# New rests for the background steps of a fused two-block kernel, and four tiles at once at the second layer's input product

## The chip, the cores and the metric

The kernel runs on one core of one Trainium2 chip. The metric is the device time of one execution in microseconds (us), the median of several runs.

## The reference

A model of two blocks on 256 positions of width 2048, in float32.

```python
# first block, two layers
mod = silu(c) @ w_ada[l] + b_ada[l]                    # shift, scale, gate
h = rms_norm(x, norm_g[l]) * (1 + scale) + shift
u, z_s, q, k, v, z_a = split(h @ w_in[l])              # 2048 x 6144
y_s = s5_mixer(u, ...) * silu(z_s)                     # state space, gelu, w_glu
y_a = diff_attention(rope(q), rope(k), v, ...) * silu(z_a)   # 8 heads
x = x + gate * (concat([y_s, y_a]) @ w_out[l])
# second block, one layer
z = rms_norm_2(x) @ w_in_2
y_rw, y_mla = rwkv7_mixer(z_rw, ...), mla_mixer(z_mla, ...)
mix = (g_rw * (y_rw @ w_branch_rw) + g_mla * (y_mla @ w_branch_mla)) @ w_out_2
h = x + rms_norm_2(mix); f = (gelu(gate) * val) @ w_down # a 3-tap convolution on w_up's product
h = h + rms_norm_2(f);   h = h + rms_norm_2(sigmoid(h @ w_ple_gate) * (p @ w_ple))
```

## The kernel before

All values are held transposed, width on the 128 partitions and the 256 positions along the row. A weight matrix is read as blocks of 128 by 128, in halves of 8 blocks (512 KB). ScalarE rounds a half to the high part of a split (beat `hi`, 1024 columns), VectorE takes the low part (`lo`), and TensorE does three matmuls of 256 columns for a block: high times high, high times low, low times high. So one block is 3 matmuls, and a tile of 128 output rows is 16 blocks where the inner width is 2048, 8 where it is 1024. The matmuls of all tiles in a row are a **stream**. TensorE's instructions have line 981 (transposes 984), ScalarE's 978, VectorE's 941 to 971, transfers 937, since helpers record them.

The order of the work is written by a planner that runs on the host, `Timeline`. It emits one list of beats, and every engine's program goes through this one list and plays its own part of each beat, in that order, waiting on semaphores. `stream` emits the blocks, and after every `per` blocks it calls `bg()`, which advances each background generator by one `yield`. `per` is 2 for the last 40 tiles of w_in, for w_outa and for the last 40 tiles of w_in2; it is 4 for the first 8 tiles of w_in, for w_glu and for w_outm. The generators are: `s5` (16 batches of the state-space scan; in each, `s5_follow` and the next batch's `s5_prepare` advance together, and every second one has `s5_phases`), `s5_back`, `attention` (8 heads of 15 steps, each head only when its four tiles are out), `modulation` (the product with w_ada for the rest of layer 0 and for layer 1, one 1 MB unit for each unit of the stream), and `rwkv` (8 head pairs of 15 steps, then 7 sequential steps `rw_seq`, then `rw_post` in 24 calls). A **rest** is the number of yields behind a step, so the number of calls until the generator's next beat. `drain` goes on calling `bg` without a stream until a generator is done.

What the steps do, for those that the change touches: in `s5_follow` step 0 TensorE multiplies by the input matrix, 1 ScalarE copies, 2 TensorE transposes, 3 VectorE rotates and scans, 4 TensorE makes y (16 small matmuls, it needs the scan and the taps `WI`, which went through DRAM, `scr_k`), 5 ScalarE copies y, 6 TensorE transposes it, 7 ScalarE copies. In `s5_prepare` 1 to 3 are VectorE's, 4 TensorE transposes, 5 ScalarE copies, 6 TensorE makes the taps, 7 ScalarE copies and POOL stores, 8 POOL loads. In `attention` 0 is the scores, 1, 2, 4 and 6 VectorE's part of the softmax, 3 and 5 ScalarE's, 7 the transposes of the weights, 8 ScalarE's copy, 9 the product with v, 10 ScalarE's squares, 11 POOL's power, 12 ScalarE's scaled copy, 13 its transposes, 14 VectorE's product. In `rwkv` step 0 is TensorE's, 1 and 2 are mostly VectorE's (decay, keys), 3 a product on TensorE and VectorE's factors behind it, 4 to 9 the inverse by doubling, 10 to 12 its application, 13 four products and VectorE's masks, 14 the last products. `s5_phase` is ten instructions of VectorE, `s5_sine` three sines on ScalarE.

The ring in SBUF has four places for halves and one of 1 MB for modulation units (places 4 and 5). SyncE's queue issues all weight loads in the order of use and waits for a place to be free before it goes on to the next.

At the boundary between the layers the last tile of w_outm is added to x, squared and summed, TensorE sums over the partitions (`rms`), ScalarE takes the root, and sixteen tiles of h are made, each by VectorE, ScalarE and VectorE. `warm` loads the table of the root ahead. A name in `PAIRS` with its first unit has the first 32 blocks in the order tile 0 k 0 to 7, tile 1 k 0 to 7, tile 0 k 8 to 15, tile 1 k 8 to 15; one in `QUADS` has the first 64 blocks as k 0 to 3 of four tiles, then k 4 to 7 of the four, and so on, and its weights are packed so (`pack_quads`).

Of the kernel before, what the change touches and what calls it, by code (L numbers as in the profile page):

```python
# [282 lines left out]

PAIRS = (("w_in", 48), ("w_in2", 0), ("w_up", 0))

QUADS = (("w_pg", 0),)


class Tile:
# [8 lines left out]
class Timeline:  # L300
# [240 lines left out]
    def s5(self, l):  # L541
        for i, parts in enumerate((1, 2, 1, 4, 3, 2, 1, 5)):
            for part in range(parts):
                self.add("s5_setup", l, i, part)
                if l or part == parts - 1:
                    yield
                if l:
                    yield
        self.add("s5_first", l)
        for x in self.s5_prepare(l, 0):  # L550
            yield
        for x in self.s5_phases(l, 0):
            yield
        while ("u8", l, 0) not in self.marks:
            yield
        for _ in range(6):
            yield
        for b in range(16):
            both = [self.s5_follow(l, b)] + ([self.s5_prepare(l, b + 1)] if b < 15 else [])
            if b % 2 and b < 15:  # L560
                both.append(self.s5_phases(l, b // 2 + 1))
            while both:
                for g in list(both):
                    if next(g, self) is self:
                        both.remove(g)
                yield
            self.marks.add(("s5", l, b))
# [23 lines left out]
                    yield  # L591

    def s5_phases(self, l, p):
        for _ in range(10 if p else 0):
            yield
        self.add("s5_phase", l, p)
        for _ in range(4):
            yield
        self.add("s5_sine", l, p)
        yield  # L600
# [9 lines left out]
            self.marks.add(("u8", l, half))  # L610

    def s5_prepare(self, l, b):
        for i, rest in enumerate((1, 2, 2, 5, 3, 4, 1, 2, 0)):
            self.add("s5_prep", l, b, i)
            for _ in range(rest):
                yield

    def s5_follow(self, l, b):
        for i, rest in enumerate((2, 3, 1, 5, 2, 3, 1, 2)):
            self.add("s5_run", l, b, i)  # L620
            for _ in range(rest):
                yield

    def attention(self, l):
        for h in range(8):
            while ("w_in", l, 8 + 4 * h + 3) not in self.marks:
                yield
            for i, rest in enumerate((2, 2, 2, 2, 2, 2, 4, 2, 2, 2, 1, 2, 2, 2, 1)):
                self.add("att", l, h, i)
                if i == 14:  # L630
                    self.add("part", ("att", l), h)
# [23 lines left out]
    def rwkv(self):  # L655
# [3 lines left out]
        for i in range(8):  # L659
            while i == 3 and ("w_in2", 0, 35) not in self.marks:  # L660
                yield
            for s, rest in enumerate((1, 2, 3, 5, 3, 3, 2, 2, 2, 2, 2, 2, 2, 2, 1)):
                slot = self.take("rw") if s in (1, 3) else None
                self.add("rw", i, s, slot)
                if slot:
# [64 lines left out]
    def run(self):  # L730
# [35 lines left out]
        for l in range(2):  # L766
# [12 lines left out]
                gy = self.s5_back(0)  # L779
                self.bgs += [g5, gy, gm]  # L780
            self.bgs.append(self.load_u8(l))
            self.mod_rest = 2
            self.stream("w_in", l, 48 * l, 0, 8, 16, per=4)
            ga = self.attention(l)
            self.bgs.append(ga)
            self.mod_rest = 5
            self.stream("w_in", l, 48 * l + 8, 8, 40, 16, per=2)
            while l == 0 and ("mod", 0, 11) not in self.marks:
                self.bg()
# [4 lines left out]
            if l == 0:  # L794
                g5, gy = self.s5(1), self.s5_back(1)
                self.bgs += [g5, gy]
            self.mod_rest = 2
            self.stream("w_glu", l, 8 * l, 0, 16, 8, per=4)
            if l:
                self.add("pos2")  # L800
# [1933 lines left out]
def arrange(i):  # L2734
    g = {k: np.asarray(v) for k, v in i.items()}
    A = {}
# [5 lines left out]
    for n, name in enumerate(("lam_q1", "lam_k1", "lam_q2", "lam_k2")):  # L2742
# [11 lines left out]
    A["w_ada"] = np.concatenate([pack_ada(w) for w in g["w_ada"]])  # L2754
    n = np.arange(8)
    order = np.concatenate([n, np.stack([16 + n, 24 + n, 32 + n, 40 + n], 1).reshape(-1), 8 + n])
    A["w_in"] = np.concatenate([pack(w.reshape(2048, 48, 128)[:, order].reshape(2048, 6144))
                                for w in g["w_in"]])
    A["w_outm"] = np.concatenate([pack(w[:1024]) for w in g["w_out"]])
    A["w_outa"] = np.concatenate([pack(w[1024:]) for w in g["w_out"]])  # L2760
    glu = g["w_glu"].reshape(2, 1024, 2, 8, 128).transpose(0, 1, 3, 2, 4).reshape(2, 1024, 2048)
# [53 lines left out]
```

How the kernel before makes its waits and increments, by code:

```python
    def then_inc(self, sem, *keys):  # L897
        p = self.port
# [15 lines left out]
    def wait_ge(self, sem, key):  # L914
        if self.e is not None:
            self.wait_value(sem, self.signals.value[sem, key])
# [1 line left out]
    def wait_value(self, sem, v):  # L918
        if self.seen.get(sem, 0) < v:
            self.e.wait_ge(self.signals.sems[sem], v)
            self.seen[sem] = v
# [65 lines left out]
def bank_ready(port, tl, before):  # L987
    if before is not None:
        sem = BANK_FREE[tl.tiles[before[1]].kind] if before[0] == "ev" else "mod_dve"
        port.wait_ge(sem, before)
# [2 lines left out]
def tile_ready(port, slot):  # L994
    i, free = slot
    if free is not None:
        port.wait_ge(*free)
    return TMP + 256 * i
# [61 lines left out]
    def mm(t, k, p, b8):  # L1061
        if k == 0:
            bank_ready(pe, tl, t.before)
        (r1, r2), key = moving(m, t.name, t.l, k)
        pe.wait_ge("rhs", key)
        pe.wait_ge("w_hi", p)
        M = 32 if (t.name, t.n) == ("w_in2", 26) else 128
        off = p % NS * 2 * HALF + b8 * 128
        o = B(t.bank, 0, 256, np_=M)
        pe.mm(o, R(off, M), r1, k == 0, False)
        pe.mm(o, R(off, M), r2, False, False)
        pe.wait_ge("w_lo", p)
        x = pe.mm(o, R(off + HALF, M), r1, False, k == t.nk - 1)
        told = [("out", t.o)] * (k == t.nk - 1) + [("half", p)] * (b8 == 7)
        if told:
            x.then_inc("mm", *told)
# [1 line left out]
    def ev(t, ph):  # L1078
# [4 lines left out]
        if t.kind in ("v", "v2") and ph == 1:  # L1083
            s = TMP + 256 * t.slots[0][0]
            pe.wait_ge("ev_act", ("ev", t.o))
            pe.tr(B(b, 256, 128), V(s, 128))
```

## Time and profile before

| | |
|---|---|
| median of 3 runs | 3167.82 us (3164.78 to 3168.11) |
| the profiled execution | 3160.48 us |
| its span | 3158.7 us |
| TensorE busy | 2928.2 us (93%) |
| VectorE busy | 2244.0 us (71%) |
| ScalarE busy | 1612.0 us (51%) |
| mean granted clock of TensorE | 0.97 |
| read from HBM | 555.22 MB |

Busy time is without waits. In the profile PE is TensorE's matmuls, PEld its weight loads, DVE VectorE, ACT ScalarE, SPq SyncE's queue; brackets say how long the engine was idle before the row, and the arrow what ended that. A row of busy time by stretch gives the stretch, its length, the busy us and the count of PE, PEld, DVE, ACT and POOL, the granted clock as a share of full speed, the share of the DMA engines and their GB/s. A timeline row has its start, the us it took, engine, line and operation.

The stages, in us from the span's start: first modulation and the first tiles of w_in to 160, the last 40 tiles of w_in of layer 0 to 573, w_outa to 641, w_glu and w_outm to 746, the boundary to 774, the first 8 tiles of w_in of layer 1 to 803, its other 40 to 1180, w_outa, w_glu, w_outm and the first 28 tiles of w_in2 to 1511, the eight head pairs of the recurrence under the other tiles of w_in2 to 1896, `rw_seq` to 1935, `rw_post` to 1966, and then the second block's attention and feed-forward part.

### The profile page before, as it was taken

What the parts mean: (1) busy time and instruction counts of PE and PEld (TensorE: products, weight loads), DVE (VectorE), ACT (ScalarE), POOL (GpSimd) and SP (SyncE); (2) the same over time, 40 slices, a digit from 0 to 9 for tenths busy, and PEclk for the clock granted to TensorE, in tenths of its full rate; (3) what the DMA queues carried; (4) which work ended last, traced back from release to release, by engine and by line L of the source; (5) the groups of instructions that cost most, each with busy time, mean ns of one, the idle gap of its engine ahead of it and who ended that gap; (6) DMA issues with size and microseconds to landing.
All of it is one profiled execution on the core that took longest, in us unless ns stands there. A gap on an engine that the chain in (4) does not pass through costs nothing.

```text
span 3158.7 us, 60121 instructions
## 1 busy us (share of the span) xinstructions
PE 2928.2 (93%) x24112; PEld 2705.5 (86%) x24112; DVE 2244.0 (71%) x3498; ACT 1612.0 (51%) x2404; POOL 286.4 (9%) x488
## 2 busy tenths in 40 slices
PE   6899998998988889999999998999899999999987
PEld 2577777787978789999888898999899999999987
DVE  6367787687788887775666667675788846887565
ACT  3335555365555655755444343645555544555454
POOL 0011221100122220300000001010000000000000
PEclk8899999998999999999999999999899999999999
DMA  9887676884645456455323334455355555555543
GB/s 375 304 260 245 231 268 219 292 277 152 180 140 160 140 159 211 163 186 163 115 97 116 106 106 132 162 179 175 129 181 185 190 186 180 182 182 173 186 147 121
DMA packets 168231, 580.97 MB, mean 184 GB/s; under 512 B 40272, under 2 KB 40304, under 8 KB 155536
## 3 DMA queue, kind: packets, MB, share of 16 engines
q1 hardware_dynamic: 146784, 525.40, 50.1%
q0 software_dynamic: 20592, 48.26, 5.0%
q8 instruction: 190, 3.11, 0.4%
q10 hardware_dynamic: 576, 3.47, 0.3%
q14 instruction: 89, 0.73, 0.1%
HBM read 555.22 MB, written 21.76 MB: 183 GB/s over the span
## 4 chain that ended last, share of the span: by engine, by line
PE 57%; DVE 24%; ACT 8%; DMA 6%; issue 3%; SPq 1%; DVEq 0%; POOL 0%; ACTq 0%
PE acc L981 57%; DVE arena L941 7%; DVE rounded L941 6%; ACT arena L978 4%; DVE upper L941 3%; ACT rounded L978 3%; DVE arena L951 2%; DMA arena<-in_w_ada 2%; DMA arena<-in_w_in 2%; DVE upper L951 1%; ACT L978 1%; ACT upper L978 1%; DMA arena<-scr_k 1%; DVE arena L967 1%; SPq L937 1%
## 5 line engine op out<-in xcount | busy, mean ns | idle before, releaser
L981 PE MATMUL acc<-rounded 128*128 128x256 f32 x14688 | 1921.7, 289 | 39.6 <-issue 14.3
L981 PEld LDWEIGHTS acc<-rounded 128*128 128x128 f32 x14688 | 1827.8, 194 | 125.5 <-issue 88.7
L941 DVE TENSOR_TENSOR rounded<-arena,rounded 128x1024 fp32r<-128x1024 f32 (+1 forms) x832 | 1004.4, 1207 | 304.2 <-ACT rounded L978 235.9
L978 ACT ACTIVATE rounded<-arena 128x1024 fp32r<-128x1024 f32 (+1 forms) x864 | 884.5, 1024 | 644.9 <-PE acc L981 422.7
L981 PEld LDWEIGHTS acc<-upper_rounded,rounded 128*128 128x128 f32 x4560 | 552.1, 193 | 22.5 <-issue 14.0
L981 PE MATMUL acc<-upper_rounded,rounded 128*128 128x256 f32 x4560 | 559.2, 284 | 6.4 <-DVE rounded L941 3.1
L978 ACT ACTIVATE arena<-arena 128x256 f32<-128x256 f32 (+4 forms) x477 | 253.5, 531 | 299.4 <-DVE arena L941 199.9
L941 DVE TENSOR_TENSOR arena<-arena 128x256 f32<-128x256 f32 (+5 forms) x458 | 244.6, 534 | 51.0 <-ACT arena L978 32.1
L981 PE MATMUL acc<-arena 128*32 128x512 f32 (+8 forms) x1550 | 215.3, 486 | 57.6 <-DVE arena L941 26.2
L951 DVE SCALAR_TENSOR_TENSOR arena<-arena 128x256 f32<-128x256 f32 (+6 forms) x465 | 209.0, 449 | 59.7 <-ACT arena L978 32.0
L941 DVE TENSOR_TENSOR arena<-acc,arena 128x256 f32<-128x256 f32 (+4 forms) x270 | 117.5, 435 | 146.8 <-PE acc L981 127.8
L978 ACT ACTIVATE arena<-acc 128x256 f32<-128x256 f32 (+3 forms) x275 | 104.1, 378 | 200.1 <-PE acc L981 180.7
L981 PE MATMUL acc<-upper 128*128 128x128 f32 (+7 forms) x1568 | 186.4, 300 | 20.2 <-DVE upper L941 10.6
L981 PEld LDWEIGHTS acc<-arena 128*32 128x32 f32 (+3 forms) x1550 | 86.9, 141 | 119.9 <-DMA arena<-in_w_ada 47.5
L981 PEld LDWEIGHTS acc<-upper 128*128 128x128 f32 (+4 forms) x1568 | 145.0, 168 | 42.3 <-DVE upper L941 13.6
L978 ACT ACTIVATE upper<-acc 128x256 f32<-128x256 f32 (+4 forms) x176 | 88.3, 502 | 139.9 <-PE acc L981 99.7
L978 ACT ACTIVATE arena<-acc,arena 128x256 f32<-128x256 f32 (+1 forms) x148 | 63.6, 429 | 85.2 <-PE acc L981 75.0
L984 PE MATMUL acc<-arena 128*128 128x128 f32 x384 | 72.3, 283 | 29.6 <-ACT arena L978 24.4
L981 PE MATMUL acc<-upper,arena 64*64 64x64 f32 (+4 forms) x482 | 63.1, 355 | 27.1 <-DVE upper L951 6.9
L937 POOL DMA_DIRECT2D arena<-scr_k x128 | 77.3, 621 | 116.6 <-DMA scr_k<-arena 115.4
L941 DVE TENSOR_TENSOR upper<-upper,acc 128x512 f32<-128x512 f32 (+2 forms) x48 | 33.1, 689 | 69.4 <-PE acc L981 68.5
L984 PEld LDWEIGHTS acc<-arena 128*128 128x128 f32 x384 | 45.2, 142 | 41.3 <-ACT arena L978 29.6
(92 smaller groups left out, 1205.6 us busy)
## 6 DMA issues: line engine op xcount, KB each, us to landing
arena<-in_w_in SPq DMA_DIRECT2D x328, 512.0 KB, 4.6
arena<-in_w_ada SPq DMA_DIRECT2D x88, 1024.0 KB, 5.6
arena<-in_w_up SPq DMA_DIRECT2D x176, 512.0 KB, 4.1
arena<-in_w_down SPq DMA_DIRECT2D x88, 512.0 KB, 4.0
arena<-in_w_outa SPq DMA_DIRECT2D x32, 512.0 KB, 6.0
arena<-in_w_glu SPq DMA_DIRECT2D x32, 512.0 KB, 6.1
arena<-in_w_outm SPq DMA_DIRECT2D x32, 512.0 KB, 4.7
arena<-in_w_out SPq DMA_DIRECT2D x32, 512.0 KB, 4.3
```

Of the source, the lines that this page charges most:

```text
L937: self.e.dma_start(out, in_).then_inc(self.signals.sems[sem], 16)
L941: return self.put(self.e and self.e.tensor_tensor(o, a, b, op))
L951: return self.put(self.e and self.e.scalar_tensor_tensor(out=o, in0=a, scalar=s, in1=b, op0=o1, op1=o2))
L967: return self.put(self.e and self.e.tensor_tensor_scan(o, a, b, 0.0, MUL, ADD))
L978: return self.put(self.e and self.e.activation(o, a, f, scale=scale, **kw))
L981: return self.put(self.e and self.e.matmul(o, l, r, start=start, stop=stop, skip_group_check=True))
L984: return self.put(self.e and self.e.transpose(o, i, self.m.con("ident")))
```

## The change

- The rests of `s5_prepare`, `s5_follow`, `s5_phases`, `attention` and `rwkv` become tables, for the first block one row for each layer, and most numbers in them differ from before.
- `mod_rest` in the last 40 tiles of w_in and in w_outa is 2 in place of 5: the calls between the asking for a modulation unit and its product.
- In layer 1, `s5_phases` of batch 0 waits until tile 0 of layer 1's w_in is out, and the scan starts 8 calls behind the load of u in place of 6.
- The second layer's w_in begins with four tiles at once (`QUADS`) in place of two (`PAIRS`), and its weights are packed for it.

```diff
-PAIRS = (("w_in", 48), ("w_in2", 0), ("w_up", 0))
-
-QUADS = (("w_pg", 0),)
+PAIRS = (("w_in2", 0), ("w_up", 0))
+
+QUADS = (("w_in", 48), ("w_pg", 0))
+
+S5_PREP = ((0, 1, 3, 6, 1, 6, 1, 2, 0),
+    (1, 2, 2, 4, 3, 3, 3, 1, 0))
+S5_RUN = ((1, 3, 1, 6, 2, 3, 2, 1),
+    (1, 4, 3, 6, 2, 1, 1, 1))
+S5_PHASE = ((13, 5),
+    (17, 2))
+S5_START = (6, 8)
+ATTENTION = ((1, 2, 4, 2, 3, 2, 4, 1, 3, 1, 1, 2, 2, 2, 1),
+    (1, 1, 2, 1, 2, 2, 4, 1, 5, 2, 2, 3, 3, 2, 1))
+RWKV = (1, 3, 3, 6, 3, 4, 2, 2, 2, 1, 2, 2, 2, 4, 1)
+MOD_REST = (2, 2, 2)
@@ def s5
+        while l and ("w_in", 1, 0) not in self.marks:
+            yield
         for x in self.s5_phases(l, 0):
             yield
         while ("u8", l, 0) not in self.marks:
             yield
-        for _ in range(6):
+        for _ in range(S5_START[l]):
             yield
@@ def s5_phases
-        for _ in range(10 if p else 0):
+        for _ in range(S5_PHASE[l][0] if p else 0):
             yield
         self.add("s5_phase", l, p)
-        for _ in range(4):
+        for _ in range(S5_PHASE[l][1]):
             yield
@@ def s5_prepare
-        for i, rest in enumerate((1, 2, 2, 5, 3, 4, 1, 2, 0)):
+        for i, rest in enumerate(S5_PREP[l]):
@@ def s5_follow
-        for i, rest in enumerate((2, 3, 1, 5, 2, 3, 1, 2)):
+        for i, rest in enumerate(S5_RUN[l]):
@@ def attention
-            for i, rest in enumerate((2, 2, 2, 2, 2, 2, 4, 2, 2, 2, 1, 2, 2, 2, 1)):
+            for i, rest in enumerate(ATTENTION[l]):
@@ def rwkv
-            for s, rest in enumerate((1, 2, 3, 5, 3, 3, 2, 2, 2, 2, 2, 2, 2, 2, 1)):
+            for s, rest in enumerate(RWKV):
@@ def run
-            self.mod_rest = 2
+            self.mod_rest = MOD_REST[0]
             self.stream("w_in", l, 48 * l, 0, 8, 16, per=4)
...
-            self.mod_rest = 5
+            self.mod_rest = MOD_REST[1]
             self.stream("w_in", l, 48 * l + 8, 8, 40, 16, per=2)
...
-            self.mod_rest = 2
+            self.mod_rest = MOD_REST[2]
             self.stream("w_glu", l, 8 * l, 0, 16, 8, per=4)
@@ def arrange
-    A["w_in"] = np.concatenate([pack(w.reshape(2048, 48, 128)[:, order].reshape(2048, 6144))
-                                for w in g["w_in"]])
+    A["w_in"] = np.concatenate([to(w.reshape(2048, 48, 128)[:, order].reshape(2048, 6144))
+                                for to, w in zip((pack, pack_quads), g["w_in"])])
```

## Rows read from the trace of the kernel before

**Rows 1.** The page, part 4: the chain that ended last, by engine.

```profile
PE 57%; DVE 24%; ACT 8%; DMA 6%; issue 3%; SPq 1%; DVEq 0%; POOL 0%; ACTq 0%
```

**Rows 2.** Busy time by stretch, with its length, clock, DMA share, GB/s.

```profile
160.00:573.00 413.00, 382.13 (x3251) 311.27 (x3250) 310.35 (x527) 216.11 (x399) 81.19 (x139) 0.97 0.75 249
...
746.00:774.00 28.00, 17.64 (x83) 14.44 (x83) 22.03 (x45) 17.75 (x29) 0.00 (x0) 0.70 0.18 57
...
803.00:1180.00 377.00, 337.36 (x2910) 305.96 (x2909) 311.93 (x527) 217.87 (x401) 82.53 (x140) 0.96 0.50 155
...
1511.00:1896.00 385.00, 364.49 (x2900) 333.61 (x2900) 240.99 (x353) 158.80 (x232) 28.10 (x52) 1.00 0.33 107
...
1896.00:1935.00 39.00, 29.82 (x527) 27.71 (x527) 31.50 (x53) 7.32 (x11) 5.48 (x8) 0.91 0.34 107
...
1935.00:1966.00 31.00, 31.00 (x277) 29.45 (x276) 18.52 (x27) 14.16 (x17) 4.53 (x7) 1.00 0.49 161
```

**Rows 3.** TensorE's waits, 160 to 573: releaser, us, times, longest.

```profile
PE acc L984 <- ACT arena L978: 7.4, 8, 2.8
...
PE acc L981 <- DMA arena<-scr_k: 6.8, 5, 2.4
```

**Rows 4.** The same, 803 to 1180.

```profile
PE acc L984 <- ACT arena L978: 17.0, 11, 4.2
...
PE acc L981 <- DVE upper L941: 8.6, 6, 2.6
```

**Rows 5.** Timeline of TensorE, one head pair of the recurrent stage.

```profile
1641.23 1.58 PE L981 MATMUL acc<-upper 128*64 128x256 f32 x16 [0.96 <-DVE upper L941]
...
1653.87 0.67 PE L981 MATMUL acc<-upper,arena 128*128 128x256 f32 x2 [1.39 <-DVE upper L951]
...
1658.71 2.10 PE L981 MATMUL acc<-arena 64*128 64x256 f32 x16 [0.58 <-DVE arena L941]
```

**Rows 6.** Timeline around the layer boundary, TensorE, VectorE, ScalarE.

```profile
738.99 0.88 DVE L941 TENSOR_TENSOR arena<-arena 128x256 f32<-128x256 f32 x2
...
741.74 4.00 PE L981 MATMUL acc<-upper_rounded,rounded 128*128 128x256 f32 x32
...
742.32 0.43 DVE L951 SCALAR_TENSOR_TENSOR arena<-arena 128x256 f32<-128x256 f32 x1
...
747.28 1.28 ACT L978 ACT_TABLE_LOAD   x1
...
748.30 0.48 DVE L951 SCALAR_TENSOR_TENSOR arena<-acc,arena 128x256 f32<-128x256 f32 x1
...
751.01 0.43 DVE L941 TENSOR_TENSOR arena<-arena 128x256 f32<-128x256 f32 x1 [2.23 <-ACT arena L978]
...
752.11 1.01 PE L981 MATMUL acc<-arena 128*128 128x1 f32 x4 [6.37 <-DVE arena L941]
...
756.66 13.99 PE L981 MATMUL acc<-rounded 128*128 128x256 f32 x63 [1.73 <-issue]
...
774.00 1.22 PE L981 MATMUL acc<-rounded 128*128 128x256 f32 x8 [0.48 <-DVE rounded L941]
```

**Rows 7.** Timeline of SyncE's queue and ScalarE in layer 0.

```profile
402.02 0.33 SPq L937 DMA_DIRECT2D arena<-in_w_ada  x1
...
402.39 1.72 SPq L937 DMA_DIRECT2D arena<-in_w_in  x2
...
409.32 1.06 ACT L978 ACTIVATE rounded<-arena 128x1024 fp32r<-128x1024 f32 x1 [3.21 <-DMA arena<-in_w_in]
```

**Rows 8.** ScalarE's waits, 160 to 573.

```profile
ACT rounded L978 <- DMA arena<-in_w_in: 97.4, 27, 8.6
```

**Rows 9.** Timeline, layer 1, one pair of attention transposes.

```profile
994.70 0.69 PE L984 MATMUL acc<-arena 128*128 128x128 f32 x2 [4.23 <-ACT arena L978]
```

**Rows 10.** Timeline of TensorE, the recurrence's last part.

```profile
1934.15 1.03 PE L981 MATMUL acc<-arena 128*128 128x256 f32 x4
...
1944.76 1.84 PE L981 MATMUL acc<-arena,upper 128*128 128x2 f32 x16
...
1954.14 1.09 PE L981 MATMUL acc<-arena,upper 128*64 128x128 f32 x16
```

## The prediction

> **What bounds the kernel now.** I read the page first: the chain that ended last lies 57% on TensorE and 24% on VectorE [rows 1], so TensorE sets the time and the rest is what makes it wait. Then the busy time by stage [rows 2]. The reader is to compare TensorE's busy time with the length of each stage: layer 0's input product leaves 413 - 382.1 = 30.9 us idle, layer 1's 377 - 337.4 = 39.6, the layer boundary 28 - 17.6 = 10.4, the recurrent stage's eight head pairs 385 - 364.5 = 20.5, its serial part 39 - 29.8 = 9.2, the part after that nothing. That is 110.6 us in all, and only a part of it can come back. The granted clock in the two products was 0.97 and 0.96 and at the boundary 0.70, with waits ahead of each fall. Then the waits of TensorE, stage by stage, to see who ends them: in layer 0 ScalarE's copies ahead of a transpose (7.4 us) and the reload of the taps (6.8) [rows 3]; in layer 1 the same copies (17.0) and VectorE's scan (8.6) [rows 4]; in the recurrent stage three places that come back with every head pair [rows 5]. Nowhere does TensorE wait long for weights: the splits run ahead.
>
> **What a rest is.** Every background step is placed in the order of all engines by counting calls of `bg`. In the big streams a call comes every 2 blocks, 6 stream matmuls or 0.72 us of stream (0.12 us each: 32 in 4.00 us [rows 6]); with the other steps' work a call lasts 413/320 = 1.3 us in layer 0 and 377/320 = 1.2 us in layer 1. A rest costs no instruction. It sets how much stream lies between a producer on ScalarE or VectorE and its reader on TensorE. All sums of the work stay the same, so an edit is worth what it takes from those idle times, or adds to them.
>
> **1. Layer 0: `MOD_REST[1]` from 5 to 2, and the new rests.** The modulation weights have one place of 1 MB. SyncE's queue waits there until the product has read it, then issues the next load and the two halves of w_in that stand behind it in order. The half in the trace landed too late: SyncE issues at 402.02 and 402.39, ScalarE's split waited 3.21 us to 409.32 [rows 7]. In the stage ScalarE waited 97.4 us in 27 times, 3.6 us each [rows 8]. Behind the split on ScalarE stand the copies for the state-space and attention steps, and TensorE's transposes wait for those. The edit moves the product 3 calls, 3.9 us, ahead of where it was, and with it the issue of those halves; that covers the 3.6. So I take away most of the 7.4 us and about a third of what else is not the taps, 16.7 us: -10. The taps' 6.8 us stays: from the last step of `s5_prepare` to the reader it is 12 calls before and after. Once, at the first product of the stage, the distance between two products is 3 calls shorter, which can cost at most 3.9 us of waiting for the modulation weights: +2. Clock: a few of its falls go, -2. Sum -10; bounds -25 (all but the taps) and +4 (nothing gained, the one wait paid in full). In the product after it (w_outa) the product again comes 3 calls earlier, but the distance from one to the next is the same, and so is that wait: 0.
>
> **2. The layer boundary.** Before, `s5_phase` of layer 1 stood on VectorE from 738.99 to 742.75, 3.8 us, while TensorE ended the stream at 745.74 (741.74 + 4.00) and the last tile was evicted only at 748.30 [rows 6]. Then `s5_sine` stood on ScalarE, with a table load of 1.28 us for the sine and a second one back, and VectorE waited 2.23 us for the squares behind it. The new wait on tile 0 of w_in moves both behind the boundary. The last eviction can then follow the stream at once (745.8 instead of 748.3, -2.5), and the square too (-2.2): the rms product comes 4.7 us before 752.11. VectorE has the 3.8 us free later, in the tiles that follow, where its splits run three halves ahead of TensorE. If that cover were gone it would cost these 3.8 us again. I take -5 with a little for the clock; bounds -7 and 0. The Trainium skill's page "ScalarE: Activation LUTs" (section "What ACT_TABLE_LOAD costs") puts a switch at about 2.66 us with its drain; by that the two loads alone would give 5.3 and this term would be about -7. The trace disagrees: the activation stood right behind the 1.28 us.
>
> **3. Quads for the second layer's first tiles.** The first stream matmul came at 756.66; sixteen tiles of h and one low split fill the 17.3 us to 774.00, about 1 us a tile [rows 6]. The old order ran k 0 to 7 of tile 0, then of tile 1, then k 8 to 15: 24 blocks were done when the stream went on at 774.00, after VectorE had given the last h and then the low split of the fourth half (in the play order that split stands behind all sixteen h). The new order needs h only to k 7 for its first 32 blocks, but its fourth half waits for the very same split. So 24 blocks again, and 774.00 (less term 2) again: 0. The data ahead of it are ready, and evictions of four tiles within 6 us find four banks. Bounds: TensorE may stand before the split and go on at the lower clock, 8 blocks of 0.36 us at half speed, +3; or the split gets ahead, -3.
>
> **4. Layer 1's rests.** `s5_follow` has 6 calls in place of 5 between the scan and the y product: the four to six waits behind 8.6 us [rows 4] lose 1.2 us each, -5. In `attention` ScalarE's square and the transposes behind it are now 8 calls apart, before 5: the transposes that waited 4.23 us at 994.70 [rows 9] and their like, -5. The other ScalarE waits: -2, clock -3. Against it: from the y product through ScalarE's copy to its transpose it was 5 calls and is 3, sixteen times; I take 0.3 us each, +5. From an attention head's scores to the transposes of its weights it was 16 calls and is 13; part of the 39.6. Sum -10; bounds -30 and +30. The state-space scan as a whole starts 2 calls later and needs 327 calls, not 335, so its back part still ends inside w_outa: 0.
>
> **5. The recurrent stage.** Each pair has 38 calls, not 34: 64 more blocks of stream lie between its steps, 23 us. They fill idle time where it is: two more calls behind step 13 cover the 0.96 us that came with all eight pairs (-7.7); one more behind step 3 covers 0.58 us and its like (-3); one more between steps 1 and 2 takes about half of waits like the 1.39 us (-3.5) [rows 5]. Sum -14 of the 20.5. But the stream has only 320 calls. The recurrence ended at call 315; now it needs 32 more, and all 24 calls of `rw_post` fall behind the stream. Before, that part took from 1934.15 to 1963.17, 29.0 us: own matmuls of 4 x 1.03 + 2 x 1.84 + 4 x 1.09 = 12.2 us [rows 10] and 16.8 us of stream, TensorE busy 31.00 of 31 us [rows 2]. Without stream its own chain through three engines shows: between 0 and 16.8 us idle. I take 7: products of one pair overlap the next one's square, but the square root and two reloads do not. Sum -7; bounds -18 (nearly all of the 20.5, no hole) and +10 (half of the 14, all 16.8). If all of the 16.8 us showed, the longer rests would cost 3 us on balance.
>
> **Sum.** -10 - 5 + 0 - 10 - 7 = -32 us. The profiled execution took 3160.5 us (span 3158.7), so 3128.5 by its own count. The median of the runs shown is 3167.8, 7.3 above it; I carry that over: **3136 us**.
>
> **Rivals.**
> *The order gives little* (12%): what TensorE no longer waits for in one place it waits for in the next, as the steps are chained; then only terms 2 and half of 5 and 1 stay, -12, 3156. For it: waits in the trace are of six kinds and 1 to 4 us, none dominates. Against it: those of rows 5 come back alike with every pair and have one cause.
> *Much more* (10%): terms 1 and 4 near their lower bounds and the clock with them, -60, 3108. For it: 110.6 us lie idle. Against: two thirds of them have no edit that is aimed at them.
> *No change to be measured* (7%): within 6 us of 3168.
> *Slower, TensorE waits more in layer 1* (9%): the 2 calls fewer around the y copy. ScalarE must give its copy within 3 calls of the y product, 2.2 us of stream or more, and when it stands in another wait (a softmax waiting for VectorE, a table load) TensorE stands too. It happens sixteen times, so it decides from 2.3 us each on, where it outweighs the other terms' -37 (-10, -5, -7 and the -15 of term 4); at 3 us each it gives +11, 3179. For it: single transposes did wait 1 to 4 us. Against: ScalarE was busy 217.9 of 377 us [rows 2], and mostly it is there before the product.
> A page of the Trainium skill, "TensorE: Matmul & The Clock Gate" (Part 1), says activity releases the throttle; by that filled gaps give speed too. The trace agrees: 0.70 at the boundary, 1.00 in the stage of rows 5.
>
> **Numbers.** Forecast (-18 to -48) 62%, and the four above. Faster by more than 0.2% (about what a measurement of this kernel can tell from no change): 62 + 12 + 10 = 84%; within: 7%; slower: 9%. The range leaves those last 16% out above, and reaches from the third case's -60 and a little more, 3095, to 3161; the forecast's own is 3120 to 3150.
>
> **What would show it.** Right: hardly any split of ScalarE waiting for w_in in layer 0, and SyncE's issues 3 calls earlier; no table load pair at the end of w_outm and the rms product within 3 us of the stream's end; no 0.96 us wait in the head pairs, and a hole with only small matmuls behind the last w_in2 tile, some 20 us long. Wrong: transposes in layer 1 that wait more than now (17.0 us), a hole of 30 us at the recurrence's end, or weight waits of TensorE in the first 64 blocks of layer 1.

## The result and the profile after

The changed kernel takes 3112.9 us (median; 3103.25 to 3115.64), the kernel before beside it 3166.3 us: a ratio of 0.9824, interval 0.9804 to 0.9844, so 53.4 us less. The profiled execution took 3103.25 us (span 3101.4), before 3160.48; both are faster than their kernels' medians, by 9.6 and 5.8 us, so what is read from the two profiles (57.2 us less) is some 4 us more than what the medians say. The range of 3095 to 3161 holds it; the forecast's own, 3120 to 3150, doesn't. It lies nearer to the rival "much more" (3108) than to 3136.

The page of the changed kernel: busy time, and the chain that ended last by engine.

```profile
PE 2908.6 (94%) x24112; PEld 2692.0 (87%) x24112; DVE 2243.8 (72%) x3498; ACT 1613.3 (52%) x2406; POOL 291.0 (9%) x488
...
PE 67%; DVE 20%; ACT 6%; DMA 4%; issue 2%; SPq 1%; DVEq 0%; POOL 0%; ACTq 0%
```

TensorE's share of the chain was 57% [rows 1] and is 67%. It is also busy 19.6 us less, 2928.2 to 2908.6, with the same work. Part of this belongs to the one execution that was profiled: in `all_w6` (below), which takes the same time, it is busy 2918.1 us.

Here and below the transposes' line is 984 before and 996 or 998 in the other kernels, and the other lines are shifted by the same 12 or 14.

To see where the 57 us of the profiled executions went, each stage was measured from its first stream matmul to that of the next stage. In us; the last three columns are kernels with one part of the change alone (told below), as differences to before. Stages that an edit doesn't touch differ by up to 6 us in layer 0 and 3.5 in layer 1, which is how far such a column can be read.

| stage | before | changed | `rests0_only` | `rests1_only` | `rwkv_only` |
|---|---|---|---|---|---|
| layer 0, last 40 tiles of w_in | 388.0 | -17.2 | -17.7 | +3.9 | +6.0 |
| layer 0, w_outa | 63.9 | -3.5 | -2.3 | +1.1 | +1.7 |
| layer 0, w_outm and the boundary | 64.8 | -5.9 | -0.5 | -1.3 | -1.1 |
| layer 1, first 8 tiles of w_in | 55.8 | +0.9 | 0.0 | -0.6 | 0.0 |
| layer 1, other 40 tiles | 357.2 | -14.4 | +2.6 | -12.7 | +1.4 |
| layer 1, w_outa | 49.5 | -2.2 | 0.0 | -2.2 | 0.0 |
| recurrence and `rw_post`, to w_up | 481.7 | -9.4 | +1.2 | +1.3 | -8.6 |

These seven give -51.7; the rest is within 2 us in any one stage. Now the two input products and the recurrence as TensorE sees them, in busy time by stretch. First the kernel before:

```profile
180.00:568.00 388.00, 361.98 (x3096) 294.96 (x3096) 298.24 (x511) 207.52 (x388) 79.88 (x137) 0.98 0.74 247
...
812.00:1170.00 358.00, 320.58 (x2759) 290.24 (x2758) 295.64 (x504) 209.20 (x389) 80.91 (x137) 0.96 0.50 150
...
1487.00:1968.00 481.00, 448.86 (x3885) 411.67 (x3885) 313.87 (x470) 193.85 (x281) 40.84 (x72) 0.99 0.34 111
```

The same stages of the changed kernel:

```profile
177.00:548.00 371.00, 356.92 (x3098) 292.75 (x3098) 296.81 (x506) 211.78 (x392) 82.73 (x136) 0.98 0.79 261
...
784.00:1127.00 343.00, 315.43 (x2775) 285.41 (x2774) 297.70 (x508) 209.99 (x389) 82.35 (x137) 0.97 0.51 156
...
1440.00:1912.00 472.00, 451.77 (x3889) 414.71 (x3887) 311.41 (x465) 193.99 (x282) 39.88 (x71) 0.98 0.35 113
```

In layer 0's product TensorE was idle 26.0 us (388 - 361.98) and is 14.1; in layer 1's 37.4 and now 27.6. That is 12 and 10 us of waits. The other 5 us of each stage is busy time, at no fewer matmuls: 361.98 to 356.92 and 320.58 to 315.43. How much of that is the clock can be read from the clock record of each trace, by how long the lower of the two levels was granted in the stage. In layer 1's product it is 30.7 us before and 20.5 now; ten us less at half speed are some 5 us of busy time (an estimate), which is what went. The eight kernels whose layer 1 wasn't touched there lie at 27.3 to 34.1 us and busy 319.3 to 322.2, the three with all its new rests (the changed one, `rests1_only`, `all_w6`) at 17.1 to 20.5 and busy 315.3 to 316.8, so this difference is clear. In layer 0's product it is 17.1 us and 13.7, worth 1.7 of the 5 us, and the seven kernels whose layer 0 wasn't touched scatter from 10.2 to 27.3 us and busy 359.7 to 365.7: there the clock's share isn't shown. The page "TensorE: Matmul & The Clock Gate" of the Trainium skill (Part 1) says that activity releases the throttle; layer 1's product agrees. The recurrence doesn't give such a gain: its waits fell too, from 32.1 us to 20.2, and its busy time rose from 448.86 us to 451.77.

TensorE's waits in layer 0's product, changed kernel: waiting and awaited, us, times, longest.

```profile
PE acc L998 <- ACT arena L992: 9.0, 5, 4.6
...
PE acc L995 <- DMA arena<-scr_k: 2.3, 1, 2.3
```

The transposes still wait for ScalarE's copies, no less than before (7.4 [rows 3]). Less is the reload of the taps, 2.3 us where it was 6.2 in the same stage (6.8 in [rows 3]), which I had left at its full size. The other kinds that wait for VectorE and ScalarE, 10.4 us in five kinds before, are gone; the wait for the modulation's weights is 2.9 where it was 1.9. The same in layer 1's product:

```profile
PE acc L998 <- ACT arena L992: 10.7, 7, 5.0
PE acc L998 <- DVE arena L965: 8.3, 5, 2.3
PE acc L995 <- DVE upper L955: 4.9, 4, 2.0
```

The transposes behind ScalarE's copies wait 10.7 where it was 15.7 in the same stage (17.0 in the longer stretch of [rows 4]) and the product behind the scan 4.9 where it was 8.6 [rows 4]. The second row has grown, from 4.2 us: the transposes of the softmax weights, which have 3 calls less.

The boundary between the layers, TensorE's timeline, changed kernel:

```profile
717.75 3.40 PE L995 MATMUL acc<-upper_rounded,rounded 128*128 128x256 f32 x27
...
722.79 0.61 PE L995 MATMUL acc<-arena 128*128 128x1 f32 x4 [1.64 <-DVE arena L955]
...
727.12 13.29 PE L995 MATMUL acc<-rounded 128*128 128x256 f32 x74 [1.72 <-issue]
744.47 15.77 PE L995 MATMUL acc<-rounded 128*128 128x256 f32 x117 [4.06 <-DVE rounded L955]
```

The rms product waits 1.64 us where it waited 6.37 [rows 6]. From the stream's end to the first matmul of the next stream it was 756.66 - 745.74 = 10.9 us and is 727.12 - 721.15 = 6.0: the 5 us of term 2. From that first matmul to the go-on behind the fourth half's low split it was 17.3 us and is 17.35: the four tiles at once change nothing of its length. They gather the idle time into one wait of 4.06 us and run the matmuls ahead of it closer, 74 in 13.29 us, where before there were three waits of 0.33, 0.48 and 0.48 us and 63 matmuls took 13.99 [rows 6].

### The profile page after: what moved, and what is told of

Its sections match the earlier page's. It is cut to its first block, busy times and chain, and to the rows that moved or that the text cites. A ratio compares the mean times of both kernels' runs of the same rounds, so it can differ in the third digit from the quotient of the medians.

```text
span 3101.4 us, 60151 instructions
## 1 busy us (share of the span) xinstructions
PE 2908.6 (94%) x24112; PEld 2692.0 (87%) x24112; DVE 2243.8 (72%) x3498; ACT 1613.3 (52%) x2406; POOL 291.0 (9%) x488
## 4 chain that ended last, share of the span: by engine, by line
PE 67%; DVE 20%; ACT 6%; DMA 4%; issue 2%; SPq 1%; DVEq 0%; POOL 0%; ACTq 0%
PE acc L995 65%; DVE arena L955 5%; DVE rounded L955 5%; DVE upper L955 2%; ACT arena L992 2%; DVE arena L965 2%; DMA arena<-in_w_ada 2%; ACT rounded L992 2%; DVE upper L965 1%; PE acc L998 1%; ACT upper L992 1%; DVE rounded L965 1%; ACT L992 1%; SPq L951 1%; DVE arena L960 0%
## 5 line engine op out<-in xcount | busy, mean ns | idle before, releaser
L955 DVE TENSOR_TENSOR arena<-arena 128x256 f32<-128x256 f32 (+4 forms) x458 | 244.6, 534 | 49.0 <-ACT arena L992 29.9
L995 PE MATMUL acc<-arena 128*32 128x512 f32 (+7 forms) x1550 | 214.2, 489 | 51.6 <-DMA arena<-in_w_ada 24.2
L965 DVE SCALAR_TENSOR_TENSOR arena<-arena 128x256 f32<-128x256 f32 (+5 forms) x465 | 208.9, 449 | 45.1 <-ACT arena L992 16.6
L955 DVE TENSOR_TENSOR arena<-acc,arena 128x256 f32<-128x256 f32 (+5 forms) x270 | 117.4, 435 | 131.0 <-PE acc L995 111.8
```

The lines of the kernel that those rows point to most:

```text
L955: return self.put(self.e and self.e.tensor_tensor(o, a, b, op))
L965: return self.put(self.e and self.e.scalar_tensor_tensor(out=o, in0=a, scalar=s, in1=b, op0=o1, op1=o2))
L995: return self.put(self.e and self.e.matmul(o, l, r, start=start, stop=stop, skip_group_check=True))
```

## The experiments

Every kernel was timed beside the kernel before, and one execution of each profiled. Unless said otherwise an edit is made to the kernel before, with everything else of the change left out. The edits of tables are shown as the numbers of all the tables in one line.

### Layer 0: the modulation's rest, or the steps' rests

`mod_only`:

```diff
-            self.mod_rest = 5
+            self.mod_rest = 2
             self.stream("w_in", l, 48 * l + 8, 8, 40, 16, per=2)
```

> The kernel before with one edit: MOD_REST[1] is 2 in place of 5. Theory: the early product lets the two halves of w_in behind the modulation load be issued 3 calls sooner, so ScalarE's 97 us of waiting for w_in in layer 0 nearly vanish; the 40 tiles of layer 0's input product take 8 to 12 us less of their 388, w_outa 2 to 4 us less of its 64, all else is unchanged. Rival: the new rests of layer 0 brought that stage's gain, and this edit alone brings under 3 us in it.

`rests0_only`, layer 0's row of all the tables:

```diff
@@ l = 0: s5_prepare, s5_follow, s5_phases, attention
-(1, 2, 2, 5, 3, 4, 1, 2, 0)  (2, 3, 1, 5, 2, 3, 1, 2)  10, 4  (2, 2, 2, 2, 2, 2, 4, 2, 2, 2, 1, 2, 2, 2, 1)
+(0, 1, 3, 6, 1, 6, 1, 2, 0)  (1, 3, 1, 6, 2, 3, 2, 1)  13, 5  (1, 2, 4, 2, 3, 2, 4, 1, 3, 1, 1, 2, 2, 2, 1)
```

> The kernel before with the new rests of layer 0 alone (S5_PREP, S5_RUN, S5_PHASE and ATTENTION row 0), MOD_REST as before. Theory: ScalarE still waits some 90 us for w_in, the stage loses 3 to 6 us of its 388, since scan and transposes get one call more. Rival: the rests are the gain and the stage loses 12 us or more here.

`scan0_only`, the same without attention's:

```diff
@@ l = 0: s5_prepare, s5_follow, s5_phases
-(1, 2, 2, 5, 3, 4, 1, 2, 0)  (2, 3, 1, 5, 2, 3, 1, 2)  10, 4
+(0, 1, 3, 6, 1, 6, 1, 2, 0)  (1, 3, 1, 6, 2, 3, 2, 1)  13, 5
```

> The kernel before with only the new scan rests of layer 0 (S5_PREP, S5_RUN, S5_PHASE row 0); attention, layer 1 and the rest as before. Theory: the scan's chain is what collides with the weights' splits, and these rests carry most of the 21 us that all rests of layer 0 brought: -12 to -18. Rival: attention's rests carry most of it, and this gives -7 or less.

| | median | ratio, interval | us |
|---|---|---|---|
| `mod_only` | 3164.57 | 0.9992, 0.9977 to 1.0007 | -2.0, not told from none |
| `rests0_only` | 3145.78 | 0.9935, 0.9911 to 0.9960 | -20.8 |
| `scan0_only` | 3149.76 | 0.9944, 0.9927 to 0.9960 | -18.3 |

ScalarE's waits in layer 0's product in `mod_only` (180 to 568):

```profile
ACT rounded L990 <- PE acc L993: 65.3, 27, 7.6
...
ACT rounded L990 <- DMA arena<-in_w_in: 10.9, 2, 6.9
```

The same waits in the kernel before (180 to 568), and then in `rests0_only` (178 to 548):

```profile
ACT rounded L978 <- DMA arena<-in_w_in: 86.5, 25, 7.6
...
ACT rounded L978 <- PE acc L981: 3.5, 4, 1.3
```

```profile
ACT rounded L990 <- DMA arena<-in_w_in: 82.8, 29, 8.5
```

The edit did what I said it does: the waits for w_in fell from 86.5 us to 10.9. The time didn't follow, because most of the idle time came back under another name: ScalarE's splits now wait 65.3 us, before 3.5, until TensorE has left their tile in `rounded`, and all of ScalarE's waits in the stage are 159.1 us where they were 160.7. ScalarE runs ahead of the stream, so it waits for something at this place in any case, and the loads were late mostly within that slack. Not wholly: TensorE's waits for ScalarE fell from 13.9 us to 9.9. But its wait for the taps rose from 6.2 us to 10.1, and in w_outa from 0.6 to 4.4, and that stage is 4.3 us longer. Why the taps come later there wasn't tried, so what the early product gives without that stays open up to those 4 us. With the new rests in place it gives nothing: TensorE is idle 14.1 us in the product in the changed kernel and 14.4 in `rests0_only`.

`rests0_only` shows the other half: the waits for w_in stay at 82.8 us, and 20.8 us of time go; I had expected 3 to 6 of the stage, and its rival (12 or more) is what happened. How these divide between scan and attention isn't settled. By the medians `scan0_only` has 18.3 of them, but the intervals reach 5 and 8 us to either side. By TensorE's idle time in the product it has about half: 26.0 us before, 20.7 in `scan0_only`, 14.4 in `rests0_only`, and 13.6 to 14.7 in the changed kernel and its three variants below. What attention's rests took away there is mostly waiting for ScalarE's copies ahead of a transpose, 15.9 us in `scan0_only` and 9.3 in `rests0_only`.

What the scan's rests took away in layer 0's product, VectorE's waits in the kernel before:

```profile
DVE arena L951 <- ACT arena L978: 20.0, 9, 4.5
DVE arena L941 <- PE acc L981: 17.3, 6, 5.6
```

and in `scan0_only` (179 to 557) the same two kinds:

```profile
DVE arena L963 <- ACT arena L990: 9.1, 5, 3.2
...
DVE arena L953 <- PE acc L993: 6.8, 4, 2.1
```

So two of VectorE's waits got shorter together: it stood 37.3 us in them and stands 15.9. Another kind grew, from 4.6 to 9.1 us, and all its waits together fell from 66.0 us to 54.1. When VectorE stands there, its splits and evictions stand behind. TensorE's list agrees in part: in `scan0_only` its waits for the taps are 0.9 us (6.2 before in the same stage), those for VectorE 1.6 (3.9), those for ScalarE's copies ahead of a transpose more, 15.9 (7.4). Which of the rests in the two rows did it wasn't tried one by one, so that these chains are the cause is argued and not shown.

### The boundary: the wait on tile 0, and the quads

`wait_only`:

```diff
+        while l and ("w_in", 1, 0) not in self.marks:
+            yield
         for x in self.s5_phases(l, 0):
```

> The kernel before with one edit: layer 1's first s5_phases waits until tile 0 of its w_in is out. Theory: the phase's 3.8 us on VectorE and the sines with their table loads on ScalarE leave the end of w_outm, which gets 4.5 to 6 us shorter; the 8 tiles behind it pay under 1 us; total -5. Rival: the boundary is set by the sixteen tiles of h and one split, and the gain is under 2 us.

`quads_only`:

```diff
-PAIRS = (("w_in", 48), ("w_in2", 0), ("w_up", 0))
-QUADS = (("w_pg", 0),)
+PAIRS = (("w_in2", 0), ("w_up", 0))
+QUADS = (("w_in", 48), ("w_pg", 0))
```

> The kernel before with one edit: layer 1's w_in begins with four tiles at once. Theory: the low split of the fourth half stands behind all h in VectorE's order, so the stream goes on at the same time as before and the first 8 tiles' stretch changes by less than 1 us. Rival 1: quads save 4 us or more of waiting for h. Rival 2: the one long wait lowers the clock and costs 1 to 3 us.

| | median | ratio, interval | us |
|---|---|---|---|
| `wait_only` | 3160.92 | 0.9981, 0.9965 to 0.9997 | -5.6 |
| `quads_only` | 3167.34 | 1.0003, 0.9987 to 1.0020 | +0.8, not told from none |

The stage with the boundary is 6.4 us shorter in `wait_only`. In `quads_only` TensorE's timeline reads:

```profile
756.83 13.21 PE L993 MATMUL acc<-rounded 128*128 128x256 f32 x74 [1.73 <-issue]
774.18 10.99 PE L993 MATMUL acc<-rounded 128*128 128x256 f32 x77 [4.13 <-DVE rounded L953]
```

774.18 against 774.00 [rows 6]: both orders have 24 blocks that they can do, and both then need the same low split. The moved steps lie under the stream of layer 1 now. ScalarE in the changed kernel, from the timeline:

```profile
760.15 1.28 ACT L992 ACT_TABLE_LOAD   x1
761.45 1.78 ACT L992 ACTIVATE arena<-arena 128x256 f32<-128x256 f32 x3
```

The activation again starts 0.02 us behind the table load, so a switch costs these 1.28 us; the 2.66 us of the Trainium skill's page "ScalarE: Activation LUTs" (section "What ACT_TABLE_LOAD costs") doesn't show. The time itself, -5.6 with an interval of -11 to -1, doesn't tell the sum from the rows (-5) from the one by the page (-7).

### Layer 1's rests

`rests1_only`, layer 1's row of all the tables:

```diff
@@ l = 1: s5_prepare, s5_follow, s5_phases, start, attention
-(1, 2, 2, 5, 3, 4, 1, 2, 0)  (2, 3, 1, 5, 2, 3, 1, 2)  10, 4  6  (2, 2, 2, 2, 2, 2, 4, 2, 2, 2, 1, 2, 2, 2, 1)
+(1, 2, 2, 4, 3, 3, 3, 1, 0)  (1, 4, 3, 6, 2, 1, 1, 1)  17, 2  8  (1, 1, 2, 1, 2, 2, 4, 1, 5, 2, 2, 3, 3, 2, 1)
```

> The kernel before with the new rests of layer 1 alone (row 1 of the tables, S5_START 8), no wait at the boundary, pairs. Theory: layer 1's 40 tiles take 12 to 16 us less of 357, as in the changed kernel, and the boundary is unchanged. Rival: part of that gain comes from the boundary edits, which bring fewer collisions, and the rests alone give under 8 us.

`scan1_only`, the same without attention's:

```diff
@@ l = 1: s5_prepare, s5_follow, s5_phases, start
-(1, 2, 2, 5, 3, 4, 1, 2, 0)  (2, 3, 1, 5, 2, 3, 1, 2)  10, 4  6
+(1, 2, 2, 4, 3, 3, 3, 1, 0)  (1, 4, 3, 6, 2, 1, 1, 1)  17, 2  8
```

> The kernel before with only the new scan rests of layer 1 (row 1 of S5_PREP, S5_RUN, S5_PHASE, and S5_START 8); attention as before. Theory: half of the 22 us of all rests of layer 1, -8 to -14; VectorE's wait of 15.0 us for ScalarE's weights of the softmax stays, since that is attention's. Rival: -18 or more, attention's new rests give nothing or take away.

`all_y3`, the changed kernel with the y copy's old distance, 5 calls, taken from the rest ahead of the scan:

```diff
 S5_RUN = ((1, 3, 1, 6, 2, 3, 2, 1),
-    (1, 4, 3, 6, 2, 1, 1, 1))
+    (1, 4, 1, 6, 2, 3, 1, 1))
```

> The changed kernel with row 1 of S5_RUN at 1 4 1 6 2 3 1 1: from the y product to its transpose 5 calls as before, in place of 3, and 1 between the copy of x and its transpose's scan. My prediction's term: layer 1 gains 3 to 5 us more. Rival: the short distance costs nothing, since ScalarE is there in time; the stage is the same within 2 us or longer, as the scan starts earlier after its transposes and waits.

`all_x1`, the changed kernel with the same rest taken away and put behind the last step, so that the y copy keeps its short distance:

```diff
-    (1, 4, 3, 6, 2, 1, 1, 1))
+    (1, 4, 1, 6, 2, 1, 1, 3))
```

> The changed kernel with row 1 of S5_RUN at 1 4 1 6 2 1 1 3: the scan comes 2 calls earlier, right behind its transposes, and the short distance from the y product to its transpose stays. Theory: all_y3 lost 6 us against the changed kernel because VectorE waits for the transposes when the scan comes right behind them, so this loses as much. Rival: it lost by the longer distance of the y copy, and this one is as fast as the changed kernel.

`all_w6`, the changed kernel with 2 calls more between the softmax and the transposes of its weights:

```diff
-    (1, 1, 2, 1, 2, 2, 4, 1, 5, 2, 2, 3, 3, 2, 1))
+    (1, 1, 2, 1, 2, 2, 6, 1, 3, 2, 2, 3, 3, 2, 1))
```

> The changed kernel with row 1 of ATTENTION at 1 1 2 1 2 2 6 1 3 2 2 3 3 2 1: the transposes of the softmax weights come 2 calls later, the product with v stays where it was. Theory: TensorE's 8.3 us of waiting for VectorE's weights in layer 1 shrink to under 3, the kernel is 3 to 6 us faster than the changed one. Rival: the wait moves to the product with v, whose copy on ScalarE now has 3 calls and not 5; no gain.

| | median, range | ratio to before, interval | us | the 40 tiles |
|---|---|---|---|---|
| `rests1_only` | 3145.19 | 0.9934, 0.9920 to 0.9949 | -21.8 | -12.7 |
| `scan1_only` | 3152.66 | 0.9953, 0.9935 to 0.9972 | -15.4 | -9.5 |
| changed kernel | 3112.89, 3103.25 to 3115.64 | 0.9824, 0.9804 to 0.9844 | -53.4 | -14.4 |
| `all_y3` | 3119.64, 3115.61 to 3120.76 | 0.9850, 0.9833 to 0.9866 | -47.4 | -4.9 |
| `all_x1` | 3124.41, 3123.15 to 3132.22 | 0.9867, 0.9850 to 0.9885 | -43.6 | +3.5 |
| `all_w6` | 3115.17, 3112.34 to 3117.66 | 0.9836, 0.9819 to 0.9852 | -52.9 | -13.1 |

`scan1_only` has 15.4 of the 21.8 us. VectorE's wait for ScalarE in this stage (its first row, 15.0 us before) was to stay there, since I took it for attention's, and fell to 3.6 us with attention's rests as before; so it was the scan's order that made it. `all_y3` was to be 3 to 5 us faster than the changed kernel by my own step for the y copy, and is 6.8 slower.

`all_x1` costs about 10 us against the changed kernel, and the intervals are apart: two calls taken from between a batch's transposes (step 2) and its rotation and scan (step 3) are worth that much. The profiled stages are 17.9 us apart: TensorE is idle 37.9 us in `all_x1`, 27.6 in the changed kernel, and 37.4 before. So without these two calls the new order of layer 1 gives nothing in its own product. Layer 1's product in `all_x1`, TensorE's waits and then VectorE's:

```profile
PE acc L998 <- ACT arena L992: 18.4, 8, 6.4
PE acc L998 <- DVE arena L965: 8.9, 4, 5.3
PE acc L995 <- DVE upper L955: 8.5, 5, 2.6
...
DVE arena L955 <- PE acc L995: 4.5, 7, 1.4
...
DVE upper L965 <- PE acc L998: 3.2, 2, 2.5
```

In the changed kernel neither of VectorE's two kinds comes to 0.5 us, and TensorE's three were 10.7, 8.3 and 4.9. VectorE comes to the rotation right behind TensorE's transposes, stands up to 2.5 us until they are done, and everything behind it comes later. Two reservations. The kernel before has this distance of 1 call too, and there the two kinds come to 1.2 us only; so the 10 us are the worth of the distance in the new order, and not what the change gained by it over the old one. And the same two calls put the scan at call 6 of a batch, right behind `s5_prepare`'s step 3 on the same engine (call 5), where it was at call 8; that this crowding has no part wasn't tried. Giving the two calls to the y copy (`all_y3`) instead of to nothing brings back 4.8 us by the medians (3124.41 - 3119.64). The first of the waits falls from 18.4 to 6.5 us, TensorE's other waits for ScalarE rise from 1.6 to 8.4, and it is idle 32.5 us in place of 37.9:

```profile
PE acc L998 <- ACT arena L992: 6.5, 4, 4.5
```

The intervals of these two overlap, so the 4.8 is a likely size and not shown apart from none; the profiled stages, 8.4 us apart, point the same way.

`all_w6` does to the softmax what its edit says, and nothing to the time:

```profile
PE acc L998 <- ACT arena L992: 10.7, 9, 5.0
PE acc L995 <- DVE upper L955: 9.5, 7, 2.0
...
PE acc L998 <- DVE arena L965: 1.3, 2, 0.9
```

The transposes' wait for VectorE falls from 8.3 us to 1.3, the one of the product behind the scan rises from 4.9 to 9.5, the others by 2.5: the list sums to 27.5 us, and to 27.4 in the changed kernel (its three rows above, and 2.4 and 1.1 us for ScalarE). VectorE has that much to do in this stage, 298 of 343 us, and what it does earlier for one reader it does later for another.

### The recurrent stage

`rwkv_only`, 38 calls for a pair:

```diff
-            for s, rest in enumerate((1, 2, 3, 5, 3, 3, 2, 2, 2, 2, 2, 2, 2, 2, 1)):
+            for s, rest in enumerate((1, 3, 3, 6, 3, 4, 2, 2, 2, 1, 2, 2, 2, 4, 1)):
```

> The kernel before with the new rests of the recurrent stage alone (38 calls a head pair, not 34). Theory: the waits of 0.96 us in front of the last step and of 0.58 us in front of step 4 vanish in all eight pairs, the eight pairs give back about 11 us and the uncovered rw_post costs about 2 us; total -9. Rival: the hole behind the stream costs 7 us and the pairs give 16.

`rwkv_34`, rests moved to the same places as far as 34 calls go:

```diff
-            for s, rest in enumerate((1, 2, 3, 5, 3, 3, 2, 2, 2, 2, 2, 2, 2, 2, 1)):
+            for s, rest in enumerate((1, 2, 3, 6, 3, 3, 2, 2, 2, 1, 2, 2, 1, 3, 1)):
```

> The kernel before with rests 1 2 3 6 3 3 2 2 2 1 2 2 1 3 1 for the recurrent stage: one call more behind steps 3 and 13, one less behind 9 and 12, 34 calls in all as before, so rw_post stays under the stream. Theory of placement: the 0.96 and 0.58 us waits shrink by 0.7 each, eight times, -8 to -10 with no hole, as good as 38 calls. Theory of amount: what counts is the 64 blocks more between the steps, and moving calls gives under 4 us, since new waits appear behind steps 9 and 12.

| | median | ratio, interval | us | stage |
|---|---|---|---|---|
| `rwkv_only` | 3157.36 | 0.9965, 0.9954 to 0.9976 | -9.6 | -8.6 |
| `rwkv_34` | 3161.89 | 0.9982, 0.9971 to 0.9993 | -5.1 | -1.8 |

The two medians are 4.5 us apart and the profiled stages 6.8; the intervals overlap a little. Both kernels are clear of the one before, so placement alone gives part of it, between the two expectations (8 to 10 us, and under 4). TensorE's idle time in the stage says the same, 32.1 us before, 26.7 in `rwkv_34` and 20.1 in `rwkv_only`. In `rwkv_34` the small waits for VectorE (the first row) are more in number, and their sum hardly falls. TensorE's waits in the stage (1493 to 1973) in `rwkv_34`:

```profile
PE acc L993 <- DVE upper L953: 13.6, 28, 2.5
PE acc L993 <- DVE upper L963: 7.0, 5, 2.4
PE acc L993 <- DVE arena L953: 3.8, 4, 2.7
```

In the changed kernel, 1440 to 1912:

```profile
PE acc L995 <- DVE upper L965: 6.9, 4, 2.6
PE acc L995 <- DVE upper L955: 6.4, 10, 2.4
PE acc L995 <- DVE arena L955: 4.5, 3, 3.2
```

Before, 1487 to 1968, the three kinds in this order were 6.9 us in 5 times, 14.8 in 17 and 9.3 in 7. A timeline of TensorE shows a head pair of the changed kernel without a wait at the places of [rows 5] (the pair before it still waits 2.56 us at the second of them):

```profile
1651.68 1.58 PE L995 MATMUL acc<-upper 128*64 128x256 f32 x16
...
1661.71 0.59 PE L995 MATMUL acc<-upper,arena 128*128 128x256 f32 x2
...
1666.59 2.10 PE L995 MATMUL acc<-arena 64*128 64x256 f32 x16
```

and the end of the recurrence, where `rw_post` now stands without stream:

```profile
1894.74 1.65 PE L995 MATMUL acc<-rounded 128*128 128x256 f32 x6
1896.19 5.12 PE L995 MATMUL acc<-arena 128*128 128x256 f32 x16
1901.15 3.63 PE L995 MATMUL acc<-arena,upper 128*128 128x2 f32 x32
1905.54 4.51 PE L995 MATMUL acc<-arena,upper 128*64 128x128 f32 x48 [0.77 <-DVE upper L973]
1910.92 1.09 PE L995 MATMUL acc<-arena,upper 128*64 128x128 f32 x16 [0.87 <-DVE arena L955]
1911.94 6.18 PE L995 MATMUL acc<-upper_rounded,rounded 128*128 128x256 f32 x50
```

From 1896.19 to 1911.94 are 15.75 us; the same matmuls had 12.2 us of their own before [rows 10]. So this part costs 3.5 us more than its own matmuls: 1.6 of idle time (0.77 and 0.87), and 1.9 of matmuls that took longer, at a granted clock of 0.80 in this stretch (see the last section).

The single edits sum to -2.0 - 20.8 - 5.6 + 0.8 - 21.8 - 9.6 = -59.0 us, the whole gives -53.4. With intervals that reach some 3 to 8 us to either side of each they agree; nothing is seen that only the whole would show. No kernel tried was faster than the changed one.

## Why the prediction was right in its sign and short in its size

**The bound** was read rightly: TensorE, and what makes it wait, in the two input products and the recurrence.

**Term 1 (-10)** had the wrong cause and half the size. The step that failed is the one from ScalarE's 97.4 us of waiting [rows 8] to the copies that stand behind the split. The wait was real and the edit removed it, but `mod_only` gives -2.0 us, not told from none: a sum of waits of an engine that is ahead is mostly slack. The 20.8 us came from layer 0's new rests, which the term has in its heading and gives no step of its own. The taps' reload, which I left at 6.8 since its count of calls stays 12, fell to 2.3; `scan0_only` has it at 0.9, so it was the scan's rests, and which chain ahead of it got shorter wasn't looked at. That w_outa would gain nothing doesn't hold for the edit alone: it lost 4.3 us in `mod_only`, most of it behind a later reload of the taps, where kernels that don't touch it differ from before by up to 1.7. In the changed kernel it is 3.5 us shorter.

**Term 2 (-5)** is -5.6 alone, and the rows show its two steps as worked out. **Term 3 (0)** is +0.8, not told from none, for the reason given. The bounds of both were never needed.

**Term 4 (-10)** is -21.8. The steps -5, -5 and -2 for longer distances are near what the waits did (the product behind the scan -3.7, the transposes behind ScalarE -5.0, its other waits -1.6). For the clock I had -3, and busy time fell 3.0 us in `rests1_only` and 4.6 in the changed kernel; the y copy's +5 is 4.8 by `all_y3` against `all_x1`. Layer 1's w_outa, which I had at 0, is 2.2 us shorter. What I left out are the pairs whose reader is VectorE: I went only through those whose reader is TensorE. The rest between the transposes and the rotation went from 1 call to 3, and in the new order that is worth some 10 us (`all_x1`). It isn't shown that this is the missing 10 us, since VectorE hardly waited there before (1.2 us); what fell most in its own list is the wait for ScalarE, from 15.0 us to 1.8, which the term didn't look at either. Which rest did that stays open. The wait for the softmax did grow, 4.2 us to 8.3 in this stage, as feared, and giving it back (`all_w6`) is worth nothing.

**Term 5 (-7)** is -9.6. The hole costs 3.5, where I took 7. The -7.7 for step 13's and -3 for step 3's places are borne out in sum: in the head pairs alone the two kinds of waits fell from 14.1 us to 2.5 (24.1 to 10.9 with `rw_seq`); the -3.5 for half of the waits of step 2 is not: they are 6.9 us before and after. The hole was to be some 20 us long and is 15.75.

**The rivals.** "Much more" came nearest, and as it said, by terms 1 and 4 near their bounds, and the clock. Its counter-argument, that two thirds of the idle time had no edit aimed at them, was wrong in that I didn't see the aim. "Slower" had the right mechanism at 0.3 us each and never came near its 2.3. "The order gives little" has a slip in its sum: term 2 and half of 5 and 1 are -13.5, not -12, which changes nothing in the argument. That rival is true of two edits tried, `mod_only` and `all_w6`, not of the whole.

## What to carry to other kernels

A long sum of waits on an engine that runs ahead has no price: look whether the wait would come back with another releaser before counting it as a gain. In an interleaved order, go through every pair of producer and reader, those between the helping engines too: a reader placed right behind its producer on another engine stops all that stands behind it in its own engine's order, and in the new order two calls there were worth 10 us where two calls at the softmax were worth nothing. And a filled gap can be worth more than its length: about a third of what the two products gained was busy time of TensorE. Don't count on it, though: in the recurrence 12 us of waits went and the busy time rose by 3.

## What was not expected of the hardware

In 1896 to 1912 of the changed kernel TensorE was busy 14.37 of 16 us and the granted clock was 0.80; in the head pairs ahead of it, under the stream, it was 1.00. Of the 3.5 us that `rw_post` took longer more than half was a lower clock and not waiting. But the lower level didn't begin there. In the changed kernel:

```profile
1885.00:1896.00 11.00, 7.80 (x90) 7.40 (x85) 8.00 (x15) 2.41 (x4) 0.56 (x1) 0.51 0.20 62
1896.00:1899.00 3.00, 3.00 (x9) 2.45 (x9) 1.84 (x4) 0.65 (x2) 0.84 (x2) 0.53 0.00 0
1899.00:1905.00 6.00, 5.78 (x42) 5.17 (x40) 2.08 (x3) 4.22 (x6) 1.14 (x2) 1.00 0.34 112
1905.00:1909.00 4.00, 3.46 (x34) 3.46 (x36) 1.73 (x4) 1.16 (x2) 0.00 (x0) 0.58 0.01 2
```

and in the kernel before, at the same places of the program:

```profile
1927.00:1934.00 7.00, 4.32 (x43) 4.28 (x44) 5.42 (x12) 0.73 (x1) 1.19 (x2) 0.51 0.27 77
1934.00:1963.00 29.00, 29.00 (x259) 27.47 (x257) 17.02 (x24) 13.97 (x17) 4.15 (x8) 1.00 0.48 153
```

In both kernels the clock fell in the last steps of `rw_seq`, behind the first of two waits of TensorE (2.45 and then 3.20 us in the changed kernel, 2.45 and 4.76 before) and with stream matmuls between them. Before, it was back at 1.00 when `rw_post` began and stayed there under the stream; now the lower level reaches some 3 us into `rw_post`. The second fall, at 1905, has nothing like it before: it lies at the wait of 0.77 us, with small matmuls alone around it. So the first fall comes with waits that both kernels have, and only the second can be the missing stream's; whether it is that or the small wait wasn't tried.
